# Differential attention beside the latent up-projections: units reordered, PSUM banks placed by hand, four heads scaled at once

## What is computed

```python
proj = h @ w_in[l]          # q_lat 384, kv_lat 256, kpe 64, dq 512, dk 512, dv 512
q  = rms_norm(q_lat, ..) @ mla_w_q_up[l]      # 4 heads of 128 + 64
kv = rms_norm(kv_lat, ..) @ mla_w_kv_up[l]    # 4 heads of 128 (k_nope) + 128 (v)
...                         # per-head rms norms, rope on the 64-wide parts
out_m = causal_attention((q_m,), (k_m,), (1.0,), v_m, MLA_QK ** -0.5)
...
out_d = causal_attention((qd[:, :, 0], qd[:, :, 1]), (kd[:, :, 0], kd[:, :, 1]),
                         (1.0, -lam), vd, DIFF_DQK ** -0.5)
out_d = rms_norm(out_d, diff_subln_g[l]) * (1.0 - lambda_init)
mixed = concatenate([out_m, out_d])
x = x + g1 * (mixed @ w_out[l])
```

## Time and profile before

| | |
|---|---|
| time, median of 3 runs | 2125.63 us (2123.16 to 2127.56) |
| profiled execution, its own time | 2128.24 us |
| its span in the trace | 2125.8 us |
| PE, DVE, ACT, POOL busy | 2006.2, 1469.1, 452.9, 1073.8 us |
| mean granted TensorE clock | 0.978 of full |

### The profile page before, as it was taken

How to read it: one execution, slowest core, us unless ns; L and a number is a source line. 1 busy time by engine, 2 the same in 40 slices (tenths; PEclk the granted TensorE clock), 3 DMA queues, 4 the chain that set the end, 5 groups by cost and what they waited for, 6 DMA issues and landing times.

```text
span 2125.8 us, 27953 instructions
## 1 busy us (share of the span) xinstructions
PE 2006.2 (94%) x10152; PEld 1477.5 (70%) x10152; DVE 1469.1 (69%) x3122; ACT 452.9 (21%) x912; POOL 1073.8 (51%) x905
## 2 busy tenths in 40 slices
PE   7999999999999998899988999999999999999796
PEld 6888866878788874578876666766666666656463
DVE  3673034333453585746998999999999899977668
ACT  4122223133453324522222010100101010010000
POOL 4344432427203743222434768666666667656562
PEclk9999999999899998999999999999999999999898
DMA  9565423524101312013337999999999999999996
GB/s 248 167 221 189 137 70 129 196 80 131 51 7 50 119 37 86 1 60 139 130 143 297 412 414 413 413 413 414 413 413 413 412 413 413 413 413 414 409 414 251
DMA packets 130071, 529.21 MB, mean 249 GB/s; under 512 B 14209, under 2 KB 18737, under 8 KB 113201
## 3 DMA queue, kind: packets, MB, share of 16 engines
q0 software_dynamic: 73728, 268.47, 31.8%
q1 hardware_dynamic: 50256, 249.05, 31.5%
q10 hardware_dynamic: 5984, 10.44, 2.1%
HBM read 520.56 MB, written 7.34 MB: 248 GB/s over the span
## 4 chain that ended last, share of the span: by engine, by line
PE 37%; DMA 27%; DVE 22%; POOL 6%; issue 6%; ACT 2%; SPq 0%; DVEq 0%; ACTq 0%; POOLq 0%
PE ps L785 26%; DMA work<-in_peer_v,consts 11%; DMA ring<-in_peer_v,consts 8%; DMA work<-in_peer_u,consts 5%; POOL work L2381 3%; POOL ring L2381 2%; DMA ring<-in_peer_u,consts 2%; PE ps L813 2%; PE ps L871 2%; DVE tables L1898 2%; DVE ring L1852 1%; DVE work L1898 1%; DVE work L1874 1%; DVE ring L1874 1%; PE ps L930 1%
## 5 line engine op out<-in xcount | busy, mean ns | idle before, releaser
L1127 PE MATMUL ps<-work,tmp 128*128 128x512 f32 x1024 | 462.3, 605 | 22.0 <-DVE tmp L1918 22.0
L2302 POOL TENSOR_TENSOR w_lo<-ring,w_hi 128x1024 fp32r<-128x1024 f32 (+2 forms) x116 | 273.9, 2367 | 394.9 <-ACT w_hi L1975 394.8
L1115 PE MATMUL ps<-hT,work 128*128 128x256 f32 x2048 | 455.4, 380 | 1.2 <-issue 1.2
L1115 PEld LDWEIGHTS ps<-hT,work 128*128 128x128 f32 x2048 | 389.9, 191 | 80.2 <-issue 30.8
L1127 PEld LDWEIGHTS ps<-work,tmp 128*128 128x128 f32 x1024 | 192.9, 193 | 245.2 <-issue 222.7
L2381 POOL DMA_INDIRECT ring<-in_peer_u,consts x136 | 178.7, 1314 | 129.0 <-DVE hT L1874 39.2
L2381 POOL DMA_INDIRECT ring<-in_peer_v,consts x138 | 173.9, 1260 | 85.6 <-issue 37.1
L785 PE MATMUL ps<-w_hi,x_hi 128*128 128x512 f32 (+2 forms) x544 | 208.5, 384 | 1.6 <-DVE tmp L1446 1.1
L785 PE MATMUL ps<-w_lo,x_hi 128*128 128x512 f32 (+2 forms) x544 | 207.3, 381 | 0.0
L1975 ACT ACTIVATE w_hi<-ring 128x1024 fp32r<-128x1024 f32 (+2 forms) x116 | 120.4, 1041 | 393.6 <-PE ps L785 284.7
L2381 POOL DMA_INDIRECT work<-in_peer_u,consts x120 | 150.8, 1257 | 77.8 <-issue 31.0
(11 more groups left out here) (329 smaller groups left out, 3102.4 us busy)
## 6 DMA issues: line engine op xcount, KB each, us to landing
work<-in_u_steps SPq DMA_DIRECT2D x64, 1024.0 KB
work<-in_peer_v SPq DMA_DIRECT2D x64, 1024.0 KB
ring<-in_a_w_in SPq DMA_DIRECT2D x48, 512.0 KB, 4.6
ring<-in_ada_w SPq DMA_DIRECT2D x48, 512.0 KB, 5.0
ring<-in_peer_w_q SPq DMA_DIRECT2D x32, 512.0 KB, 3.5
ring<-in_a_w_out SPq DMA_DIRECT2D x16, 512.0 KB, 4.2
ring<-in_b_w_in SPq DMA_DIRECT2D x16, 512.0 KB, 4.3
ring<-in_c_in SPq DMA_DIRECT2D x12, 512.0 KB, 3.9
```

The costliest lines, as they stand in the source:

```text
L1115: mm = pe.matmul(ps[:, 4 + s, j * DT:(j + 1) * DT], u_ring[:, s, j, k, :], hT[:, k, GATHERED * P:T], start=(k == 0), stop=(k == KD - 1))
L1127: mm = pe.matmul(ps[:, 2 * t + half, :], tmp[:, s, j * DT + t * P:j * DT + (t + 1) * P], v_ring[:, s, j, half * BANK:(half + 1) * BANK], s ...
L2302: pool.tensor_tensor(w_lo[q % NPIECE][:, 0:n], ring[:, at:at + n], w_hi[q % NPIECE][:, 0:n], ALU.subtract).then_inc(w_split, 1)
```

## The change

- The latent transposes move from behind the last projection chunk to ahead of the dk chunk; ACT takes them to SBUF instead of DVE.
- `qdT` and `kpeT` are taken by ACT instead of DVE, and so are `qnT` and `qrT`.
- The units start with the eight d units of heads 0 and 1, with `k_nope` and `v_up` of one token tile in each of the first four steps, and the 40 transposes `qnT`, `knT`, `qrT` in steps 4 to 8 (`TURNED`). 24 units follow, as m, d, m.
- The transposes of the probabilities lag 3 steps instead of 2, the product with v 6 instead of 4, and it comes last in a step.
- DVE writes negated scores and their minimum, so that the negation is gone; ACT's exponential has a scale of -1.
- A d output is clamped straight into SBUF and freed; `att_scale` scales the four heads of a query tile in one instruction, 4 times in all.
- The split of the first four `c_out` weight pieces moves from one block ahead of attention into it, a piece at a time, on ACT and on POOL.
- Banks are placed by hand in this stage, in the rotation's order named A3, B2, B3, A2, A0, A1, B0, B1. Some buffers move.

```diff
-ATT_LAG = 4
+ATT_PT, ATT_LAG, ATT_END = 3, 6, 3
+ATT_FIRST = 8
+ATT_ROWS = (3, 1, 2, 0)
+TURNED = {4: (("qnT", 0), ("qnT", 1)), 5: (("qrT", 0), ("qnT", 2)), 6: (("knT", 0), ("knT", 1)),
+          7: (("knT", 2), ("knT", 3)), 8: (("qnT", 3), ("qrT", 1))}
...
-    for n in C_CHUNKS:
+    for n in range(3):
         for t in range(NT):
             jobs.add("c_in", n, t)
+    A3, B2, B3, A2, A0, A1, B0, B1 = ((jobs.turn + i) % NB for i in range(NB))
+    for i in range(3):
+        jobs.put((A3, B2, B3)[i], "qlT", i)
+    for i in range(2):
+        jobs.put((A2, A3)[i], "kvlT", i)
+    for t in range(NT):
+        jobs.put((B2, B3, A2, A3)[t], "c_in", 3, t)
+    for t in range(NT):
+        jobs.put((A0, A1, B0, B1)[t], "c_in", 4, t)
     jobs.skip(NT)
...
+        jobs.put((A0, B0, B2, A2)[t], "q_nope", t)
+        jobs.put((A1, B1, B3, A3)[t], "q_rope", t)
     for h in range(DIFF_H):
...
+        jobs.put((A0, B0, A1, A0)[h], "qdT", h)
+        jobs.put((A1, A0, B0, A1)[h], "kdT", h)
+    jobs.put(B0, "kpeT", 0)
+    units = [("d", n // NT, ATT_ROWS[n % NT]) for n in range(ATT_FIRST)]
+    for n in range(ATT_FIRST):
+        h, i = n // 2, n % 2 * 2
+        units += [("m", h, i), ("d", 2 + n // NT, ATT_ROWS[n % NT]), ("m", h, i + 1)]
+    scored = 0
     for n in range(len(units) + ATT_LAG):
         if n < len(units):
-            jobs.add("att_s", n, 0)
-            if units[n][0] == "d":
-                jobs.add("att_s", n, 1)
+            for c in range(2 if units[n][0] == "d" else 1):
+                jobs.put((A0, A1, B0)[scored % 3], "att_s", n, c)
+                scored += 1
+        if n < NT:
+            jobs.put((B2, B3)[n % 2], "k_nope", n)
+            jobs.put(B1, "v_up", n)
+        for c, key in enumerate(TURNED.get(n, ())):
+            jobs.put((B2, B3)[c], *key)
+        if ATT_PT <= n < len(units) + ATT_PT:
+            jobs.put(B1 if n % 2 or n <= max(TURNED) else B3, "att_pT", n - ATT_PT)
         if n >= ATT_LAG:
-            jobs.add("att_o", n - ATT_LAG)
-        if 2 <= n < len(units) + 2:
-            jobs.add("att_pT", n - 2)
+            jobs.put((A2, A3, B2)[n % 3 if n > max(TURNED) else n % 2], "att_o", n - ATT_LAG)
...
-        c_od = [W(0, 512), W(512, 512), tables[:, 2048:2560], tables[:, 2560:3072]]
-
-        d_xn, d_qT = W(0, NT, D), W(23552, 4, DT)
+        c_od = [W(7168, 512), ysum, tables[:, 2048:2560], tables[:, 2560:3072]]
+        c_sq = [tables[:, 3968:4096], ones]
...
+                if n == 3:
+                    for i in range(3):
+                        transposes(("qlT", i), lambda t: c_ql[:, t, i * P:(i + 1) * P],
+                                   lambda t: drained(pe, "c_in", 0, t))
+                    for i in range(2):
+                        transposes(("kvlT", i), lambda t: c_kvl[:, t, i * P:(i + 1) * P],
+                                   lambda t: drained(pe, "c_in", 1, t))
...
+                if n == 0:
+                    for ii in range(2):
+                        drained(pe, "kvlT", ii)
+                    for p in range(2):
+                        arrived(pe, "kv_up", 0, p)
+                if n < NT:
+                    tokens_by_features(("k_nope", n), c_kvlT, kv_w, 2, 0, 512, n)
+                    tokens_by_features(("v_up", n), c_kvlT, kv_w, 2, 512, 512, n)
+                for what, hh in TURNED.get(n, ()):
...
+                if k >= 4:
+                    pe.wait_ge(od_scaled, NT)
...
+                    if n >= 16:
+                        dve.wait_ge(at_rl, n - 15)
                     taken(dve.tensor_tensor_reduce(
                         out=c_s[:, sl, 0:N], in0=o[:, 0:N], in1=mask,
-                        scale=float((NOPE + ROPE) ** -0.5 if kind == "m" else ROPE ** -0.5), scalar=LOWEST,
-                        op0=ALU.add, op1=ALU.max, accum_out=astat[:, c, n % 16:n % 16 + 1]), "att_s", n, c)
-                    drained(dve, "att_s", n, c)
-                    if n >= 16:
-                        dve.wait_ge(at_rl, n - 15)
-                    dve.tensor_scalar(astat[:, 2 + c, n % 16:n % 16 + 1], astat[:, c, n % 16:n % 16 + 1], -1.0, None,
-                                      ALU.mult).then_inc(at_nm, 1)
+                        scale=-float((NOPE + ROPE) ** -0.5 if kind == "m" else ROPE ** -0.5), scalar=HIGHEST,
+                        op0=ALU.add, op1=ALU.min, accum_out=astat[:, c, n % 16:n % 16 + 1]), "att_s", n, c)
...
             def att_clamp(n):
                 kind, h, i = att_units[n]
                 if kind == "d":
-                    u = diff_before[n]
                     o = full(dve, "att_o", n)
-                    if u >= 2:
-                        dve.wait_ge(od_sq, u - 1)
-                    dve.tensor_scalar(tmp[:, u % 2, 0:P], o[:, 0:P], BIG, -BIG, ALU.min, ALU.max).then_inc(od_clamped, 1)
+                    taken(dve.tensor_scalar(c_od[i][:, h * P:(h + 1) * P], o[:, 0:P], BIG, -BIG, ALU.min, ALU.max),
+                          "att_o", n)
 
             def att_out(n):
                 kind, h, i = att_units[n]
                     o = full(dve, "att_o", n)
                     taken(dve.tensor_scalar(c_om[i][:, h * P:(h + 1) * P], o[:, 0:P], astat[:, 6, at], None,
                                             ALU.mult), "att_o", n)
...
-            for n in range(n_units + ATT_LAG + 1):
+
+            def att_scale(n):
+
+
+                kind, h, i = att_units[n]
+                at = slice(i * DIFF_H, (i + 1) * DIFF_H)
+                dve.wait_ge(od_r, diff_before[n] + 1)
+                dve.scalar_tensor_tensor(rstat[:, 2, at], rstat[:, 0, at], SUM_MAX, rstat[:, 2, at],
+                                         ALU.is_le, ALU.mult).then_inc(od_rr, 1)
+                dve.wait_ge(od_rr, ATT_ROWS.index(i) + 1)
+                y = c_od[i].rearrange("p (h d) -> p h d", d=P)
+                for hh in range(DIFF_H):
+                    drained(dve, "att_o", att_of["d", hh, i])
+                dve.tensor_tensor(y, y, rstat[:, 2, at].unsqueeze(2).to_broadcast([P, DIFF_H, P]),
+                                  ALU.mult).then_inc(od_scaled, 1)
+
+            for n in range(n_units + ATT_LAG + ATT_END):
                 if n < n_units:
                     att_scores(n)
+                if 1 <= n <= NT:
+                    hn_reduce(HN_PROJ + 8 + n - 1)
                 if 1 <= n <= n_units:
                     att_norm(n - 1)
+                if 1 <= n <= NT:
+                    hn_scale(HN_PROJ + 8 + n - 1, c_dst(HN_PROJ + 8 + n - 1))
                 if ATT_LAG <= n < n_units + ATT_LAG:
                     att_clamp(n - ATT_LAG)
-                if n > ATT_LAG:
+                if ATT_LAG < n <= n_units + ATT_LAG:
                     att_out(n - ATT_LAG - 1)
+                m = n - ATT_LAG - ATT_END
+                if m >= 0 and att_units[m][0:2] == ("d", DIFF_H - 1):
+                    att_scale(m)
...
+                    if chunk == 2 and t == 2:
+                        for i in range(3):
+                            o = full(act, "qlT", i)
+                            taken(act.activation(c_qlT[:, i, :], o, ACT.Copy, scale=col("qlat_g", i)), "qlT", i)
+                        for i in range(2):
+                            o = full(act, "kvlT", i)
+                            taken(act.activation(c_kvlT[:, i, :], o, ACT.Copy, scale=col("kvlat_g", i)), "kvlT", i)
...
             for h in range(DIFF_H):
+                o = full(act, "qdT", h)
+                taken(act.activation(c_qdT[:, h, :], o, ACT.Copy), "qdT", h)
                 o = full(act, "kdT", h)
                 taken(act.activation(c_kdT[:, h, :], o, ACT.Copy), "kdT", h)
...
+            o = full(act, "kpeT", 0)
+            taken(act.activation(c_kpeT[:], o, ACT.Copy), "kpeT", 0)
             n_units = len(att_units)
             for n in range(n_units + ATT_LAG):
                 if n < n_units:
...
-                        act.wait_ge(at_nm, use + 1)
+                        drained(act, "att_s", n, c)
...
+                if n < NT:
+                    hn_square(HN_PROJ + 8 + n)
+                    o = full(act, "v_up", n)
+                    taken(act.activation(c_v[:, n, :], o, ACT.Copy), "v_up", n)
+                for what, h in TURNED.get(n, ()):
+                    o = full(act, what, h)
...
+                if n >= ATT_FIRST and n % 3 == 0:
+                    high_parts(split_at["c_out", 0, 0] + min((n - ATT_FIRST) // 3 + 1, NPIECE))
...
-            low_parts(split_at["c_out", 0, 0] + NPIECE)
             for u in range(DIFF_H * NT):
+                if u % 2 == 1:
+                    low_parts(split_at["c_out", 0, 0] + min(max(u - 3, 0) // 2, NPIECE))
                 pool.wait_ge(od_sq, u + 1)
+                kind, h, i = [unit for unit in att_units if unit[0] == "d"][u]
+                at = slice(i * DIFF_H + h, i * DIFF_H + h + 1)
```

More of the change, by code:

```diff
@@ L63 @@
 LOWEST = -3.0e38
+HIGHEST = 3.0e38
 SQ_SCALE = 2.0 ** -32
@@ L551, in network @@
         lam_act = sem("lam_act")
-        at_nm = sem("at_nm")
```

(13 more changed lines are left out.)

173 lines of the change are left out of this document (60 added, 113 removed).

## The result

| | before | after |
|---|---|---|
| median (lowest to highest), 4 runs each | 2124.77 us (2123.16 to 2127.56) | 2102.96 us (2102.00 to 2103.97) |
| ratio, 95% interval | | 0.9896 (0.9879 to 0.9913) |
| profiled execution, span | 2128.24, 2125.8 us | 2102.45, 2100.5 us |

A forecast was written before the change was run, and what follows sets the result against it. PE was taken to bound the kernel, its stage of 144.0 us losing 19.1 to waits and 13.5 to half clock. Waits 4.4, POOL -1.0 and clock 7.0 sum to 10.4 us: median 2125.6 to about 2115, range 2107 to 2124.

The forecast's parts named there:

- Latents sooner: Latent transposes ahead of the dk chunk: PE waits 1.3 us there for ACT's copies; the old 2.3 us wait goes.
- ahead of the first unit: 36 transposes before the first scores, over three banks that ACT alone empties: wait of 1.4 us instead of 3.3.
- steps 0 to 3: Attention's first steps, with the kv up-projection: PE leads DVE; one shared bank, B1, costs 0.8 us of wait.
- step 4: `qnT` 1 needs bank B3, still holding `k_nope` 3 until DVE frees it: PE waits 3.7 us.
- the end: End of attention: `att_scale` follows the last output while PE has 16 transposes; wait of 0.2 us instead of 1.6.
- Steps 4 to 15: ACT has more work than PE: 3.3 us of further waits in steps 4 to 8, 2.5 in 9 to 15.
- The rest of attention: Later attention steps: the 7.6 us of PE waits go, with 1.5 us kept.
- Clock: Half clock in the stage: 6.5 us lost (4.5 behind step 4, 2 elsewhere) instead of 13.5, so 7.0 won.
- the slower rival: Half clock from the first `k_nope` to step 9, about 34 us of PE work: 7 us slower, 2133; chance 0.09.
- PE's work is the same: PE's work in the changed stage stays 111.4 us at full clock; only waiting and clock can change.
- POOL beside DVE: Four low parts on POOL beside `att_norm` can hold up DVE: 1 us charged, between 0 and 9.2.
- the clock stays up: Rival: through attention only one short drop, 2 us lost instead of 6.5; gain 14.9 us, about 2111; chance 0.20.

The follow-up runs named there:

- y1: Kernel before, with only d outputs clamped into SBUF and the four heads of a query tile scaled in one instruction; median 2112.98 us, ratio 0.9932.
- y3: Kernel before, with only the lags changed: transposes of the probabilities 3 steps behind, product with v 6 and last in a step; ratio 0.9992.
- x1: Changed kernel with two tiles in other banks, `k_nope` 3 in A3 and `v_up` 3 in A2; median 2096.42 us, ratio 0.9857.
- x4: Changed kernel with the first four `c_out` weight splits back in one block each on ACT and POOL; ratio 0.9929, 223.3 us from `c_in` to `c_out`.
- y4: Kernel before, with scaling over four heads, the longer lags with the product last, and negated scores; 2117.22 us, ratio 0.9949.

## Why the prediction was right in direction and half the size

*What bounds the kernel* was right: waits and half clock, 19.6 and 13.7 us in the stretch. The gain came from these two.

*Latents sooner* (1.3 us of wait forecast, 0.9 measured), *ahead of the first unit* (1.4, 0.4), *steps 0 to 3* (0.8, 0.7), *step 4* (3.7, 3.5, by DVE's L1346 as named) and *the end* (0.2, 0.7) were right in place and near in sum, 7.4 forecast and 6.2 measured; the size ahead of the first unit was not. y1 and y3 bear out that the old waits stood in a chain through POOL.

*Steps 4 to 15* is the step that failed: 3.3 and 2.5 us of waits "ACT-bound" did not come. I had summed 16.7 us of ACT for steps 4 to 8 and 15.3 for 9 to 15. ACT over these two stretches (fourth figure, after PE, PEld and DVE):

```profile
825.21:843.77 18.56, 15.12 (x93) 11.64 (x93) 11.11 (x39) 13.22 (x39) 4.03 (x11) 0.82 0.07 29
843.77:858.04 14.27, 14.27 (x80) 9.01 (x79) 9.79 (x40) 13.01 (x42) 10.25 (x18) 1.00 0.18 43
```

13.2 and 13.0 us. I had taken every d step at the price of one with 512 keys, 0.72 us an exponential, while these steps have 128, 256 and 384 too, at 0.40, 0.50 and 0.61 us. The exponentials measured 4.8 and 5.9 us where I had 7.2 and 7.5, which is most of the difference. PE's side, 12 and 14.5, was near: 18.56 us less the wait of 3.5 and the 3.4 of half clock is 11.7 for steps 4 to 8, and steps 9 to 15 took 13.9. So ACT had 1.5 us more than PE in the first five steps, which the wait and the half clock of step 4 covered (x1, without them, has 1.7 us of waits for ACT there), and less than PE in the next seven. x4 shows how near the limit it was: 3.92 us of ACT in one block is 3.5 us of PE.

*The rest of attention*: 1.5 us of waits kept by guess, 0.1 measured. The chain's own rows gave no reason to keep any; y4 has none either. Together with the ACT steps, 7.3 us of the 14.7 were not there.

*Clock*: 6.5 us forecast to be lost, 3.4 were. The place was right, behind step 4 (4.5 forecast), the "one shorter drop elsewhere" did not come, for the waits that would have led to it did not either. Against 13.7 us in the stretch before, 10.3 were won instead of 7.0. It also fell to this term that the slower rival, half clock through the mixed steps, did not come: from 804 to 844 us 6.8 us ran at half clock, not 34.

*PE's work is the same* was wrong by 3.1 us: the same matmuls had 3 us less of busy time. In attention it fell as its waits did (84.0 - 7.6 - 9.8 = 66.6 before, 65.6 in y1, 63.0 in y4). Why was not measured.

*POOL beside DVE*: 1.0 charged, nothing paid. The four low parts stood at 849.30, 854.10, 859.75 and 871.99 us for 2.36 us each, and the L1572 of these steps began at 853.22, 858.12 and 870.54, between them. None was over 0.75 us. That is luck of this order, not absence of the mechanism, as x4's 2.72 us show.

In sum: 12.6 of waits instead of 4.4, 10.3 of clock instead of 7.0, 3.1 of work instead of 0, and 0 instead of -1.0 for POOL: 26.0 us in the stretch instead of 10.4. The medians show 21.8, since the profiled execution of before lies 3.5 us above its median. The chance of "faster by more" adds up to 0.75, not to 0.76. Of the rivals "the clock stays up" was nearest, and short for the same reason.
